# Expert down projection as three F32R products, with later row-number copies, a scatter without padding rows and an earlier first search

## The chip, the cores and the metric

The kernel runs on one core of a Trainium2 chip. The metric is the device time of one execution in microseconds. Three executions of the kernel before gave a median of 2249.87 us (2245.90 to 2253.77).

## What is computed

The reference is one layer of a decoder trunk over 1024 tokens of 1024 channels in float32: token mixers, a layer norm, a mixture of experts, a second layer norm. The change lies in the mixture of experts:

```python
N_EXPERTS = 64; TOP_K = 6; D_EXPERT = 256; D_MODEL = 1024
x = layer_norm(ALPHA * x + mix)                   # 1024 tokens
scores = sigmoid(x @ router_w.T)                  # (1024, 64)
gate, eidx = 6 experts of each token, weights that sum to 2.5
y[token] = shared(x)[token] + sum over its 6 experts e of
    gate * ((silu(x @ wg[e]) * (x @ wu[e])) @ wd[e])   # 1024 -> 256 -> 1024
x = layer_norm(ALPHA * x + y)
```

So there are 6144 pairs of a token and an expert. Each expert has 3 MB of weights: `wg` and `wu` of 1 MB each, and `wd` of 1 MB.

## The kernel before

**Stages.** The mixers and their merge fill the first 1100 us or so; they are not changed. `back` holds the rest: the output projection and first layer norm with the router (to about 1222 us), the tables of the routing and the shared expert of the first four token tiles (to 1275), the expert loop (to 2176), and a tail with the shared expert of the last four tiles (`shared_up(4)` to `shared_up(7)`, `tail_down`) and the second layer norm.

**Blocks.** The rows of each expert are cut into blocks of 128. There are 76 blocks, numbered b, with two buffer slots (s = b % 2). Block b passes through these steps:

- `one_hots(b)` (VectorE, L1987) compares positions with ranks; `find(b)` (TensorE, L1577) multiplies that with token numbers and weights; `rows(b)` (VectorE, L1992 to L2005) turns the result into row numbers `idx` and row weights. Rows past the expert's count get the number r + 1024, a padding row.
- `gather(b)` (GpSimd, L1429): an indirect DMA of the rows from `x1d`. It has a bound of S - 1, past which rows are not moved.
- `turn(b)` (TensorE, L1539) transposes the rows; ScalarE copies them out (L1739).
- `up(b)` (TensorE, L1550): eight float32 products of 512 columns, in two parts of four; ScalarE makes the silu (L1746), VectorE the product (`hide`, L2018).
- The transposes of `hidden` (TensorE, L1698), and a ScalarE copy to `hid_t` (L1824).
- `down(b)` (TensorE, L1564): four float32 products of 512 columns; copies of the two halves to `y_out` by ScalarE (L1835) and VectorE (L2034).
- The scatter (GpSimd, L1473): an indirect DMA that adds the 128 rows of `y_out` into `acc` in DRAM. It has no bound: `acc` has 128 rows more for the padding rows. Each waits until the one before has landed, as two experts may hold one token.

**Order.** Each engine runs a program of its own, written out by hand, and they meet in semaphores. TensorE's body of block b is: transposes of hidden(b), `up(b+1)` part 0, `find(b+3)`, `up(b+1)` part 1, `turn(b+2)`, `down(b)`. VectorE's is: `rows(b+3)`, `hide(b+1)`, `one_hots(b+4)`, the copy of half of y. At the end of `hide(b+1)` VectorE waits until scatter b-1 has landed, and copies the row numbers to `idx_out` (L2021). ScalarE's is: `hid_t`, silu of b+1, the copy of `turn(b+2)`, the copy of half of y. GpSimd's is: `gather(b+3)`, scatter b.

**Weights.** SyncE loads `w_gu` (both up matrices) and `w_d` of an expert into rings of four slots. The load for expert k+3 is issued when the last `up` of expert k-1 is done, that of `w_d` for k+2 when the last `down` of k-2 is done. `up_landed` and `down_landed` tell TensorE that a slot is filled.

**Before the loop.** TensorE interleaves the shared expert of tiles 0 to 3 with the tables. GpSimd adds each tile's result to the scaled x (L1452) and stores it to `acc` (L1454); only after the fourth store has landed does it issue `gather(2)`, which `turn(2)` waits for, and `down(0)` stands behind `turn(2)`. `find(0)` and `find(1)` stand behind the third shared transposes.

**After the loop.** The last two bodies are written out. Between them TensorE runs `shared_up(4)` (L1510), and in the last body `shared_up(5)` before `down`. VectorE runs `tail_hidden(4)` and `tail_hidden(5)` (L2049) before its own last body.

Of the kernel before, what the change touches and what calls it, by code (L numbers as in the profile page):

```python
# [18 lines left out]
P = 128  # L19
D = 1024  # L20
S = 1024
KD = D // P
NT = S // P
# [1202 lines left out]
def back(nc, d, c_at, merged, w_out, work, rings_at, half_merged, wo_in, piece_in, consts_moe, x1d, acc, x1, out, sem):  # L1226


    with ExitStack() as ctx:
# [6 lines left out]
        cst, rb, sh = sb('e_const', [P, consts_moe.shape[1]]), sb('rb', [P, E]), sb('sh', [P, 6144])  # L1236
# [6 lines left out]
        def const(name):  # L1243
# [17 lines left out]
        s_acc = y_out  # L1261
        x_gt = work[:, 2048:4096].rearrange('p (s k c) -> p s k c', s=2, c=P)
# [24 lines left out]
        scored, counted = sem('scored'), sem('counted')  # L1287
# [23 lines left out]
                  (ht_ready, 1))  # L1311
# [10 lines left out]
        def _(sp):  # L1322
# [60 lines left out]
            for t in range(NU, NT):  # L1383
                sp.wait_ge(x_scaled, t - NU + 1)
                sp.dma_start(acc[t * P:(t + 1) * P, :], x1_n[:, t, :]).then_inc(acc_rest, 16)
            sp.wait_ge(s_y, NU)
            load_up(2, 2)
            load_down(2, 2)
            up_landed(0, 0)
            up_landed(1, 0)  # L1390
# [3 lines left out]
            down_landed(0, 0)  # L1394
# [7 lines left out]
            for k in range(E - 4, E):  # L1402
                step(k, k % 4, k // 4)

# [16 lines left out]
        def _(pool):  # L1421
# [25 lines left out]
            for t in range(NU):  # L1447
                s = t % 2
                if t + 1 in (1, 3):
                    shared_hidden(t + 1)  # L1450
                pool.wait_ge(s_y, t + 1)
# [13 lines left out]
            def body(b, s, ahead=True):  # L1465
                if ahead:
# [3 lines left out]
                pool.wait_ge(so_ready, b + 1)  # L1470
# [3 lines left out]
                                        in_=y_out[:, s, :], in_offset=None, compute_op=ALU.add  # L1474
# [16 lines left out]
        def _(pe):  # L1491
# [13 lines left out]
            def shared_up(t, part=None):  # L1505
# [3 lines left out]
                for k in range(KD) if part is None else range(4 * part, 4 * part + 4):  # L1509
                    ins = pe.matmul(bank[s][:, :], turned_x1(t)[:, k, :], s_gu[:, k, :], start=k == 0, stop=k == KD - 1)  # L1510
# [45 lines left out]
            def down(b, s, e):  # L1556

                pe.wait_ge(d_landed, e + 1)
# [586 lines left out]
```

## Time and profile before

| | before |
|---|---|
| median of three executions | 2249.87 us |
| profiled execution, its own time | 2247.61 us |
| span of the profiled execution | 2245.6 us |
| TensorE busy | 95% of the span |
| mean granted TensorE clock | 0.98 |
| VectorE, ScalarE, GpSimd busy | 44%, 23%, 22% |
| DMA | 391.6 MB, 174 GB/s over the span; 297 GB/s from 1350 to 2150 us |

The profile is one execution. A trace row tells when an instruction began, how long it took and what its engine had waited for. In the chain of waits, pieces of TensorE are paced by the distance from one matmul to the next, and are thus shorter than the sum of the durations, since matmuls overlap. A float32 product appears as two matmul records.

### The profile page before, as it was taken

To read this page: it belongs to the slowest core of one execution; us is meant where nothing else is said; L and a number is where in the kernel's file an instruction comes from. 1 tells how busy PE (TensorE), PEld (TensorE's weight loads), DVE (VectorE), ACT (ScalarE), POOL (GpSimd) and SP (SyncE) were. 2 spreads that over 40 slices of the span, in tenths; PEclk is the share of its full clock that TensorE was granted. 3 is DMA by queue.
4 is the path that set the end of the run, shared out by engine and by line. 5 is a ranking of instruction groups with operands and counts; after the bars stand their busy time and mean duration, and the time that the engine had idled before them with its cause. 6 is when DMAs were issued, how large, how long until landed. Compare 5 with 4: busy or idle time off the path is not lost. (4 is left out here: it accounts for less than half of the span.)

```text
span 2245.6 us, 30409 instructions
## 1 busy us (share of the span) xinstructions
PE 2135.6 (95%) x9137; PEld 1340.0 (60%) x9138; DVE 984.2 (44%) x2409; ACT 525.6 (23%) x1056; POOL 493.0 (22%) x341
## 2 busy tenths in 40 slices
PE   7999999899999999689999799999999999999995
PEld 5887777677786666468455345455455555454542
DVE  2694525443076777388367222222222222222226
ACT  2111212342123444310132211211222112111213
POOL 2342232233132210012000312122222221222113
PEclk8999999999999999899999899999999999999998
DMA  5122221224322110377603578999888989888844
GB/s 174 47 67 89 71 66 29 80 52 101 102 80 74 48 43 17 106 234 241 227 28 132 196 227 278 331 329 336 293 291 283 327 287 325 280 288 294 261 83 159
DMA packets 162926, 391.62 MB, mean 174 GB/s; under 512 B 22272, under 2 KB 92193, under 8 KB 138144
## 3 DMA queue, kind: packets, MB, share of 16 engines
q1 hardware_dynamic: 127328, 294.88, 35.5%
q0 software_dynamic: 26304, 78.92, 16.4%
q10 hardware_dynamic: 9216, 16.78, 2.0%
q8 instruction: 49, 0.80, 0.2%
q14 instruction: 29, 0.24, 0.0%
HBM read 329.70 MB, written 75.50 MB: 180 GB/s over the span
## 5 line engine op out<-in xcount | busy, mean ns | idle before, releaser
L1550 PE MATMUL e_bank<-w_gu,work 128*128 x1216 | 553.1, 598 | 2.4 <-SPq L1338 1.7
L538 PE MATMUL a_bank<-x_hi,w_hi 128*128 128x512 f32 x928 | 375.7, 405 | 9.0 <-DVE x_lo L898 9.0
L538 PE MATMUL a_bank<-x_hi,w_lo 128*128 128x512 f32 x928 | 365.2, 394 | 0.0
L538 PE MATMUL a_bank<-x_lo,w_hi 128*128 128x512 f32 x928 | 364.9, 393 | 0.0
L1550 PEld LDWEIGHTS e_bank<-w_gu,work 128*128 128x128 f32 x1216 | 219.6, 190 | 222.2 <-issue 221.7
L1564 PE MATMUL e_bank<-w_d,norm 128*128 x608 | 274.9, 595 | 0.0
L1473 POOL DMA_INDIRECT acc<-work,idx_out x76 | 120.1, 1581 | 642.6 <-issue 613.6
L538 PEld LDWEIGHTS a_bank<-x_hi,w_hi 128*128 128x128 f32 x928 | 176.6, 190 | 50.4 <-issue 13.4
L538 PEld LDWEIGHTS a_bank<-x_hi,w_lo 128*128 128x128 f32 x928 | 176.3, 190 | 38.5
L538 PEld LDWEIGHTS a_bank<-x_lo,w_hi 128*128 128x128 f32 x928 | 176.7, 190 | 34.6 <-issue 0.5
L1564 PEld LDWEIGHTS e_bank<-w_d,norm 128*128 128x128 f32 x608 | 110.6, 192 | 110.8 <-issue 110.8
L481 POOL CAST w_hi<-w_raw 128x1024 fp32r<-128x1024 f32 x56 | 65.0, 1162 | 489.5 <-PE a_bank L538 489.5
L1746 ACT ACTIVATE norm<-e_bank 128x256 f32<-128x256 f32 x76 | 29.1, 383 | 500.3 <-PE e_bank L1550 500.3
L483 POOL TENSOR_TENSOR w_lo<-w_raw,w_hi 128x1024 fp32r<-128x1024 f32 x56 | 145.0, 2589 | 4.6
L1987 DVE TENSOR_TENSOR one_hot<-e_const,x 128x1024 bf16 x78 | 95.5, 1225 | 112.6 <-issue 112.6
L2018 DVE SCALAR_TENSOR_TENSOR norm<-e_bank,row_gate,norm 128x256 f32<-128x256 f32 x76 | 36.7, 484 | 236.4 <-ACT norm L1746 236.4
L1502 PE MATMUL e_bank<-work 128*128 128x512 f32 x256 | 113.1, 600 | 4.2 <-issue 4.2
L1539 PEld LDWEIGHTS e_bank<-e_const,work 128*128 128x128 f32 x608 | 79.4, 191 | 41.4 <-issue 36.1
L1429 POOL DMA_INDIRECT work<-x1d,idx x77 | 80.2, 1042 | 87.0 <-DVE idx L2005 47.3
L918 DVE SCALAR_TENSOR_TENSOR reg_b<-reg_b,conv_p 128x1024 f32<-128x1024 f32 x60 | 98.2, 1712 | 0.0
L836 ACT ACTIVATE reg_a<-a_bank 128x512 f32<-128x512 f32 (+2 forms) x106 | 58.5, 552 | 155.3 <-PE a_bank L545 153.7
L1739 ACT ACTIVATE work<-e_bank 128x512 f32<-128x512 f32 x152 | 82.5, 595 | 43.0 <-PE e_bank L1539 43.0
(331 smaller groups left out, 2442.8 us busy)
## 6 DMA issues: line engine op xcount, KB each, us to landing
w_d<-in_moe_wd SPq DMA_DIRECT2D x64, 1024.0 KB, 8.5
w_gu<-in_moe_wg SPq DMA_DIRECT2D x64, 1024.0 KB, 7.0
w_gu<-in_moe_wu SPq DMA_DIRECT2D x64, 1024.0 KB, 9.2
w_raw<-in_w_in SPq DMA_DIRECT2D x54, 512.0 KB, 3.8
gates<-gate_out ACTq DMA_DIRECT2D x64, 256.0 KB, 2.0
g_sb<-gates SPq DMA_DIRECT2D x16, 1024.0 KB, 6.2
work<-in_w_out SPq DMA_DIRECT2D x4, 1024.0 KB, 9.1
x<-in_x SPq DMA_DIRECT2D x8, 512.0 KB, 12.1
```

The lines of the kernel that those rows point to most:

```text
L481: pool.tensor_copy(w_hi[:, c % 2, :, :], w_raw[:, c % 2, :, :]).then_inc(w_hi_ready, 1)
L483: pool.tensor_tensor(w_lo[:, c % 2, :, :], w_raw[:, c % 2, :, :], w_hi[:, c % 2, :, :].bitcast(F32), ALU.subtract).then_inc(w_lo_ready, 1)
L538: ins = pe.matmul(bank[h][:, :], w[:, c % 2, k, :], x[:, k, cols], start=(k == 0 and j == 0), stop=(k == KD - 1 and j == 2))
L918: ins = dve.scalar_tensor_tensor(conv_y[:, c, :], conv_h[:, c, k:k + S], conv_p[:, c, k:k + 1], conv_y[:, c, :], ALU.mult, ALU.add)
L1429: pool.indirect_dma_start(out=x_g[:, s, :], out_offset=None, in_=x1d[:, :], in_offset=bass.IndirectOffsetOnAxis(ap=idx[:, s:s + 1], axis=0 ...
L1473: pool.indirect_dma_start(out=acc[:, :], out_offset=bass.IndirectOffsetOnAxis(ap=idx_out[:, s:s + 1], axis=0), in_=y_out[:, s, :], in_offs ...
L1502: ins = pe.matmul(bank[2 * (t % 2) + h][:, :], merged[:, k, t * P:(t + 1) * P], w_out[:, k, h * HALF:(h + 1) * HALF], start=k == 0, stop=k ...
L1539: ins = pe.transpose(bank[4 + k // 4][:, (k % 4) * P:(k % 4 + 1) * P], x_g[:, s, :].rearrange('p (c k) -> p k c', k=KD)[:, k, :], ident)
L1550: ins = pe.matmul(bank[s][:, :].rearrange('p (m f) -> p m f', m=2), x_gt[:, s, k, :], w_gu[:, bass.ds(e & 3, 1), :, k, :].rearrange('p a m ...
L1564: ins = pe.matmul(bank[2 + h][:, :], hid_t[:, j, :], w_d[:, bass.ds(e & 3, 1), j, h * HALF:(h + 1) * HALF].rearrange('p a f -> p (a f)'), ...
L1739: ins = act.activation(x_gt[:, s, 4 * h:4 * h + 4, :], bank[4 + h][:, :].rearrange('p (k c) -> p k c', k=4), ACT.Copy)
L1987: dve.tensor_tensor(one_hot[:, s, :, :], bcast(ranks, 1, NT), pos[:, :, bass.ds(e, 1)].broadcast_to([P, NT, P]), ALU.is_equal).then_inc(oh ...
```

## The change

- The shared expert's matrices are loaded a second time before the tail, into ring slots of the last experts (`tail_gu`, `tail_d`), and their old place `sh` is given to `d_hi`, `d_lo`, `h_hi` and `h_lo`, all of type F32R. (`tail_gu` is 2 MB, `tail_d` 1 MB.)
- `down(b)` becomes, for each of its four products, three F32R products: high x high, high x low, low x high. ScalarE copies `w_d` to `d_hi` (two copies of 128x1024) and the transposed hidden to `h_hi`; VectorE subtracts for `d_lo` (two of 128x1024) and `h_lo` (128x256). TensorE waits for `d_lo_ready` and `ht_ready`, and no longer loads the expert number for `down` into a register; ScalarE and VectorE now do.
- The copy of row numbers to `idx_out` moves from `hide(b+1)` to the end of body b, behind `one_hots(b+4)`, and waits for the scatter of b-2.
- The scatter gets the bound S - 1.
- `find(0)` and `find(1)` move forward, between the two parts of `shared_up(3)`, with the register loads; GpSimd makes each shared hidden product one tile earlier and issues `gather(0)` and `gather(1)` before it waits for tile 1's result; SyncE announces the first weights before it waits for the shared expert.

```diff
-        scored, counted = sem('scored'), sem('counted')
+        scored, tail_in = sem('scored'), sem('tail_in')
+        d_hi_ready, d_lo_ready, h_hi_ready = sem('d_hi_ready'), sem('d_lo_ready'), sem('h_hi_ready')
...
+            up_landed(0, 0)
+            up_landed(1, 0)
+            down_landed(0, 0)
             sp.wait_ge(s_y, NU)
             load_up(2, 2)
             load_down(2, 2)
-            up_landed(0, 0)
-            up_landed(1, 0)
             load_down(3, 3)
             sp.wait_ge(acc_rest, 16 * (NT - NU))
             load_up(3, 3)
-            down_landed(0, 0)
...
                 step(k, k % 4, k // 4)
+                if k == E - 3:
+                    sp.wait_ge(gu_blocks, blocks_until(E - 4) + 2)
+                    for i, name in enumerate(('sh_wg', 'sh_wu')):
+                        sp.dma_start(tail_gu[:, :, i * FE:(i + 1) * FE], d[name][0].rearrange('(k p) f -> p k f', p=P)
+                                     ).then_inc(tail_in, 16)
+                if k == E - 2:
+                    sp.wait_ge(gu_blocks, blocks_until(E - 3) + 2)
+                    sp.dma_start(tail_d, d['sh_wd'][0].rearrange('(k p) n -> p k n', p=P)).then_inc(tail_in, 16)
...
-                if t + 1 in (1, 3):
+                if t + 1 < NU:
                     shared_hidden(t + 1)
+                if t == 1:
+                    pool.wait_ge(x1_stored, 16 * NT)
+                    for k in range(2):
+                        gather(k, k)
                 pool.wait_ge(s_y, t + 1)
...
                 pool.dma_start(acc[t * P:(t + 1) * P, :], s_acc[:, s, :]).then_inc(acc_in[s], 16)
-                if t == 1:
-                    shared_hidden(2)
-                    pool.wait_ge(x1_stored, 16 * NT)
-                    for k in range(2):
-                        gather(k, k)
...
-                pool.wait_ge(so_ready, b + 1)
+                pool.wait_ge(so_ready, b + 2)
...
-                                        in_=y_out[:, s, :], in_offset=None, compute_op=ALU.add
+                                        in_=y_out[:, s, :], in_offset=None, bounds_check=S - 1, oob_is_err=False,
+                                        compute_op=ALU.add
                                         ).then_inc(scattered, 16)
...
-            def down(b, s, e):
-
-                pe.wait_ge(d_landed, e + 1)
+            def down(b, s):
+
+                pe.wait_ge(d_lo_ready, 2 * b + 2)
                 pe.wait_ge(ht_ready, b + 2)
...
                 for h in range(2):
+                    cols = slice(h * HALF, (h + 1) * HALF)
                     for j in range(2):
-                        ins = pe.matmul(bank[2 + h][:, :], hid_t[:, j, :],
-                                        w_d[:, bass.ds(e & 3, 1), j, h * HALF:(h + 1) * HALF
-                                            ].rearrange('p a f -> p (a f)'), start=j == 0, stop=j == 1)
+                        for i, (x, w) in enumerate(((h_hi, d_hi), (h_hi, d_lo), (h_lo, d_hi))):
+                            ins = pe.matmul(bank[2 + h][:, :], x[:, j, :], w[:, j, cols], start=j == 0 and i == 0,
+                                            stop=j == 1 and i == 2)
                 ins.then_inc(d_blocks, 1)
...
             shared_turn(1)
-            shared_up(3)
+            shared_up(3, 0)
+            n = trips(pe)
+            e_first = [expert_of(pe, blk) for blk in range(3)]
+            find(0, 0, e_first[0])
+            find(1, 1, e_first[1])
+            shared_up(3, 1)
             shared_down(1)
             shared_turn(2)
-            n = trips(pe)
-            find(0, 0, expert_of(pe, 0))
-            find(1, 1, expert_of(pe, 1))
             shared_down(2)
...
             body(2 * n, 0, n, ahead=False)
+            pe.wait_ge(tail_in, 48)
             shared_up(NU)
...
+            def down_high(b, e):
+
+                act.wait_ge(d_landed, e + 1)
+                act.wait_ge(d_blocks, b + 2)
+                for j in range(2):
+                    act.activation(d_hi[:, j, :], w_d[:, bass.ds(e & 3, 1), j, :].rearrange('p a f -> p (a f)'), ACT.Copy
+                                   ).then_inc(d_hi_ready, 1)
+
             def body(b, s, ahead1=True, ahead=True):
+                down_high(b, expert_of(act, b))
                 act.wait_ge(ht_done, b + 3)
-                act.wait_ge(d_blocks, b + 2)
-                act.activation(hid_t[:, :, :], bank[6][:, 0:2 * P].rearrange('p (j c) -> p j c', j=2), ACT.Copy
-                               ).then_inc(ht_ready, 1)
+                act.activation(h_hi, bank[6][:, 0:2 * P].rearrange('p (j c) -> p j c', j=2), ACT.Copy
+                               ).then_inc(h_hi_ready, 1)
...
-                dve.wait_ge(scattered, 16 * blk + 16)
-                dve.tensor_copy(idx_out[:, s:s + 1], idx_kept[:, s:s + 1]).then_inc(so_ready, 1)
+
+            def down_low(b, e):
+
+                for j in range(2):
+                    dve.wait_ge(d_hi_ready, 2 * b + j + 1)
+                    dve.tensor_tensor(d_lo[:, j, :], w_d[:, bass.ds(e & 3, 1), j, :].rearrange('p a f -> p (a f)'),
+                                      d_hi[:, j, :].bitcast(F32), ALU.subtract).then_inc(d_lo_ready, 1)
+                dve.wait_ge(h_hi_ready, b + 1)
+                dve.tensor_tensor(h_lo, bank[6][:, 0:2 * P].rearrange('p (j c) -> p j c', j=2), h_hi.bitcast(F32),
+                                  ALU.subtract).then_inc(ht_ready, 1)
 
             def body(b, s, ahead1=True, ahead=True):
+                down_low(b, expert_of(dve, b))
                 if ahead:
                     rows(b + 3, 1 - s)
...
                 if ahead:
                     one_hots(b + 4, s)
+                dve.wait_ge(scattered, 16 * b + 16)
+                dve.tensor_copy(idx_out[:, s:s + 1], idx_kept[:, s:s + 1]).then_inc(so_ready, 1)
                 dve.wait_ge(d_blocks, b + 3)
-                dve.wait_ge(scattered, 16 * b + 16)
                 dve.tensor_copy(y_out[:, s, HALF:D], bank[3][:, :]).then_inc(y_dve, 1)
```

## Rows read from the trace of the kernel before

**Rows 1.** Part 1 of the page: busy us (share of the span) x instructions.
```profile
PE 2135.6 (95%) x9137; PEld 1340.0 (60%) x9138; DVE 984.2 (44%) x2409; ACT 525.6 (23%) x1056; POOL 493.0 (22%) x341
```
**Rows 2.** Chain of waits, 1950 to 1963 us: start us, us, what.
```profile
1950.29 3.44 PE e_bank L1564 x8
1953.73 0.23 PE e_bank L1698 x2
1953.95 3.44 PE e_bank L1550 x8
...
1957.57 3.54 PE e_bank L1550 x8
1961.11 0.89 PE e_bank L1539 x8
```
**Rows 3.** Timeline, silu copies of two blocks: start us, us, engine line op [idle <-releaser].
```profile
1308.85 0.38 ACT L1746 ACTIVATE norm<-e_bank 128x256 f32<-128x256 f32 x1 [6.43 <-PE e_bank L1550]
...
2161.86 0.38 ACT L1746 ACTIVATE norm<-e_bank 128x256 f32<-128x256 f32 x1 [6.43 <-PE e_bank L1550]
```
**Rows 4.** Timeline, F32R products of the mixer stage.
```profile
299.96 0.39 PE L538 MATMUL a_bank<-x_hi,w_hi 128*128 128x512 f32 x1
...
302.90 0.39 PE L538 MATMUL a_bank<-x_lo,w_hi 128*128 128x512 f32 x1
```
**Rows 5.** Chain of waits, 1500 to 1530 us.
```profile
1508.64 7.75 DMA acc<-work,idx_out
...
1516.41 0.07 DVE idx_out L2021
...
1520.88 2.93 DMA acc<-work,idx_out
```
**Rows 6.** DMA queues, 1450 to 1550 us: packets, MB, share of 16 engines.
```profile
q1 hardware_dynamic: 3547, 25.77, 63.2%
q0 software_dynamic: 2429, 7.13, 36.7%
```
**Rows 7.** Issue to landing: the scatter (L1473), then the gather (L1429).
```profile
DMA to landing us min/median/max: 6.0/7.2/9.9
...
DMA to landing us min/median/max: 2.9/7.5/11.4
```
**Rows 8.** One line's instructions: copy (L1186) and subtraction (L1206) to F32R, ns min/median/max.
```profile
L1186 ACT ACTIVATE y_hi<-work x8: 1037/1058/1915, 945.7 to 963.5; 128x1024 fp32r<-128x1024 f32 x6, 128x2048 fp32r<-128x2048 f32 x2
L1206 DVE TENSOR_TENSOR y_lo<-work,y_hi x8: 1218/1226/3975, 946.8 to 965.9; 128x1024 fp32r<-128x1024 f32 x6, 128x2048 fp32r<-128x2048 f32 x2
```
**Rows 9.** Timeline of one block, 1956 to 1962 us.
```profile
1958.35 0.27 DVE L2005 TENSOR_SCALAR idx<-idx_f,found,e_const 128x1 int32<-128x1 f32 x1
1960.89 1.04 POOL L1429 DMA_INDIRECT work<-x1d,idx  x1 [3.19 <-issue]
```
**Rows 10.** Timeline of the last one-hots before the loop, then the chain of waits.
```profile
1242.90 1.22 DVE L1987 TENSOR_TENSOR one_hot<-e_const,x 128x1024 bf16 x1 [0.65 <-issue]
...
1259.47 6.44 PE e_bank L1529 x8
...
1274.95 9.11 DMA acc<-work
...
1285.85 9.26 DMA work<-x1d,idx
```
**Rows 11.** Timeline in the tail, end of `shared_up(5)`.
```profile
2190.48 3.60 PE L1564 MATMUL e_bank<-w_d,norm 128*128 x8
2190.74 0.38 ACT L1813 ACTIVATE norm<-e_bank 128x256 f32<-128x256 f32 x1 [6.44 <-PE e_bank L1510]
2191.22 0.42 DVE L2049 TENSOR_TENSOR norm<-e_bank,norm 128x256 f32<-128x256 f32 x1 [6.68 <-ACT norm L1813]
```
**Rows 12.** Timeline, a small VectorE instruction beside GpSimd's addition.
```profile
1272.32 2.33 POOL L1452 TENSOR_TENSOR work<-work 128x1024 f32<-128x1024 f32 x1 [1.97 <-ACT work L1804]
...
1272.52 2.15 DVE L2002 SCALAR_TENSOR_TENSOR idx_f<-found,e_const 128x1 f32<-128x1 f32 x1
```

More of the change, by code:

```diff
@@ L1235, in back @@
         scores = sb('scores', [P, NT, E])
-        cst, rb, sh = sb('e_const', [P, consts_moe.shape[1]]), sb('rb', [P, E]), sb('sh', [P, 6144])
+        cst, rb = sb('e_const', [P, consts_moe.shape[1]]), sb('rb', [P, E])
+        sh_at = (nc.sbuf_base + 31) // 32 * 32
+        sh = sb('sh', [P, 6144])
+        assert nc.sbuf_base == sh_at + 4 * 6144
         x1_late = sb('x1_late', [P, NT - NU, KD, P])
@@ L1261, in back @@
         s_acc = y_out
+        tail_gu = w_gu[:, 0, :, :, :].rearrange('p m k f -> p (m k f)').rearrange('p (k f) -> p k f', k=KD)
+        tail_d = w_gu[:, 1, 0, :, :].rearrange('p k f -> p (k f)').rearrange('p (k n) -> p k n', k=2)
+        d_hi, d_lo, h_hi, h_lo = (nc.alloc_sbuf_tensor_at(name, [P, 2, n], F32R, offset=sh_at + at) for name, n, at in (
+            ('d_hi', D, 0), ('d_lo', D, 8 * D), ('h_hi', P, 16 * D), ('h_lo', P, 16 * D + 8 * P)))
+        d_hi, d_lo, h_hi, h_lo = d_hi[:, :, :], d_lo[:, :, :], h_hi[:, :, :], h_lo[:, :, :]
         x_gt = work[:, 2048:4096].rearrange('p (s k c) -> p s k c', s=2, c=P)
@@ L1310, in back @@
         CREDIT = ((gu_blocks, 2), (d_blocks, 2), (h_ready, 2), (ht_done, 2), (y_act, 1), (y_dve, 1), (xt_done, 1),
-                  (ht_ready, 1))
+                  (ht_ready, 1), (so_ready, 1))
         def trips(eng):
@@ L1509, in shared_up @@
                 for k in range(KD) if part is None else range(4 * part, 4 * part + 4):
-                    ins = pe.matmul(bank[s][:, :], turned_x1(t)[:, k, :], s_gu[:, k, :], start=k == 0, stop=k == KD - 1)
+                    ins = pe.matmul(bank[s][:, :], turned_x1(t)[:, k, :], (s_gu if t < NU else tail_gu)[:, k, :], start=k == 0,
+                                    stop=k == KD - 1)
                 if part != 0:
@@ L1636, in tail_down @@
                         ins = pe.matmul(bank[2 + 2 * (t % 2) + h][:, :], tail_t[:, t % 2, j, :],
-                                        s_d[:, j, h * HALF:(h + 1) * HALF], start=j == 0, stop=j == 1)
+                                        tail_d[:, j, h * HALF:(h + 1) * HALF], start=j == 0, stop=j == 1)
                 ins.then_inc(s_down, 1)
@@ L1682, in _ @@
             turn(0, 0, 16)
-            find(2, 0, expert_of(pe, 2))
+            find(2, 0, e_first[2])
             for part in range(2):
-                up(0, 0, expert_of(pe, 0), part)
+                up(0, 0, e_first[0], part)
             pe.wait_ge(s_y, NU)
@@ L1708, in body @@
                     up(b + 1, 1 - s, e_up, 1)
-                e_down = expert_of(pe, b)
                 if ahead:
                     turn(b + 2, s, 16 * i + 32)
-                down(b, s, e_down)
+                down(b, s)
             turn(1, 1, 16)
@@ L1999, in rows @@
                     dve.wait_ge(xt_done, blk)
+                    if not isinstance(blk, int):
+                        dve.wait_ge(so_ready, blk - 2)
                     keep_rows(s)
@@ L2026, in body @@
                 elif ahead1:
+                    dve.wait_ge(so_ready, b + 1)
                     keep_rows(1 - s).then_inc(idx_ready, 1)
```

## The prediction

> **What bounds the kernel now.** I read page part 1 first: TensorE is busy 95% of the span, the next engine half as much [rows 1]. The share alone doesn't say whether the expert loop waits for something, so I read the chain of waits over one block next [rows 2]. The pieces touch each other: 3.44 us for `down`, 0.23 for the hidden transposes, 3.44 and 3.54 for the two parts of `up`, with 0.18 for `find` between them, 0.89 for `turn`. Their starts run from 1950.29 to 1961.11 + 0.89 = 1962.00, a period of 11.71 us, and all of it is TensorE. How often is a block longer? The silu copies mark each block; from 1308.85 to 2161.86 lie 72 periods [rows 3], 853.0 us, where 72 x 11.706 would be 842.8. So TensorE paces the loop, and all other waits in it cost 10.2 us together.
>
> Those 10.2 us come from a ring that is as long as the block. In the chain around 1500 us a scatter is issued at 1508.64 and takes 7.75 us; then VectorE copies row numbers at 1516.41, does `one_hots` and its half of y, and GpSimd issues the next scatter at 1520.88, 12.24 us after the one before [rows 5]. Just there the DMA engines are full: 63.2% of their time for weights and 36.7% for gather and scatter [rows 6]. So the block has three limits close together: TensorE at 11.71, the scatter ring at about 12.2 when transfers are slow, and the transfers themselves. The question is which of them is next once TensorE is faster.
>
> **The products.** F32R products of 512 columns start 0.226 us apart in the mixer stage: 13 steps from 299.96 to 302.90 [rows 4]. The new `down` has 4 x 3 = 12, so 2.71 us in place of 3.44 [rows 2]: 0.73 us less. For 76 blocks that is 55.5 us, all on the path. Bounds: none of these sits in a mixture of float32 and F32R instructions of this form; if each `down` paid one unhidden start of a product (0.39 - 0.23 = 0.16 us more), 12 us would be lost. I take none, as the two row types are alike in shape.
>
> **What feeds them.** Per block ScalarE makes two copies of 128x1024 at 1.05 us and VectorE two subtractions at 1.22 us [rows 8], and 0.42 us for `h_lo` (as the tail's product of that size [rows 11]). All instructions of this can begin only when the previous `down` is done, since `d_hi` and `d_lo` have one buffer. Counted from the start of `down(b-1)`: it ends at about 3.0 (2.71 and 0.3 until the next engine starts), the y copies are issued, a register load for the expert number takes some 0.8 (estimate: from 1516.41 to the next scatter's issue are 4.5 us [rows 5]; less 1.22 for `one_hots` [rows 10], 0.7 for the y copy and 1 to issue, 1.6 are left for two such loads), so `d_hi` is made from 3.8 to 5.9, `h_hi` to 6.2, `d_lo` from 4.9 to 7.3, `h_lo` to 7.7. TensorE wants them at 10.98, after transposes, `up`, `find` and `turn`. The cover is 3.3 us, so I cost this at nothing. If it is gone, each microsecond past it is a microsecond per block. Behind the new waits on VectorE stands `rows(b+3)`, about 1.0 us (to 8.7), then `hide(b+1)`, which can't run before the silu at about 10.5: 1.8 us of room. Behind `rows` stands the gather. Before, row numbers were ready at 1958.62 and `down` began at 1961.83 by its first record, 3.2 us later; now it is 2.3. And `turn(b+3)` wants the rows one period later, which is 0.73 shorter. The gather had 11 to 13 us between its issue (1960.89 [rows 9]) and its `turn`; it will have about 10 to 11.5. It lands after 7.5 us in the median, 11.4 at most [rows 7]: most fit, a few don't. I cost these at 3 us in all (bounds 0, and 1 us for each of the 45 or so blocks that run with full DMA engines).
>
> **The copy of row numbers.** Moved behind `one_hots` and waiting for the scatter of b-2, it leaves the ring. What is left of the ring is the landing, 7.2 to 9.9 us [rows 7], and about 1 us to issue, against 10.98. `so_ready` now comes one block later for GpSimd, but 0.15 us before the y copy, which it waits for anyway. So the 10.2 us mostly go: 10.2 less the 3 for gathers is a gain of 7.
>
> **No padding rows.** Scatters carry 76 x 128 = 9728 rows, of which 6144 are real. The transfers between 1450 and 1550 us took 36.7 us of all engines for 7.13 MB, 5.1 us per MB [rows 6]; 3584 rows of 4 KB are 14.7 MB, so about 75 us of the DMA engines' time, 1.0 us per block. None of it is on the path now. Its worth is that it keeps the transfers out of the way: in that stretch a block with new weights takes 63.2/8.19 = 7.7 us for weights (25.77 MB at 3.15 MB per expert are 8.19 experts) and 36.7/8.24 = 4.5 us for rows, together 12.2; without some 45 padding rows it is 11.3 by this price, against a new TensorE period of 10.98. Two facts soften that: 76 blocks share 64 loads, and the ring of four slots lets the loads run two or three experts ahead. Over the loop the sum is 64 x 7.7 + 76 x 3.5 = 759 us against 76 x 10.98 = 834. I cost it at nothing, with the rival below.
>
> **Before the loop.** Now TensorE gets to `find(0)` at 1256.21, because it first waits for GpSimd's hidden product of tile 2, which stands behind tile 1's result. In the new order that product needs only the silu of tile 2, and the searches can start as soon as the one-hots are there: the second were made from 1242.90 to 1244.1 [rows 10]. Stepping through the new order with the durations of the trace (`down` of a tile 3.44 us and half an `up` 3.54 [rows 2], ScalarE's copies 1.05 [rows 8], GpSimd's addition 2.33 [rows 12]), TensorE does find(0), find(1) by 1246, the second half of `shared_up(3)` by 1249.5, `shared_down(1)` by 1253, (2) by 1258, (3) by 1263.5, and GpSimd stores tile 3 at 1267.4, where it was 1274.95 [rows 10]. That is 7.5 us earlier; part of it is `shared_down(2)`, which took 6.44 us at a reduced clock after idling [rows 10] and would take 3.44. The chain behind it, 9.11 us for the store and 9.26 for `gather(2)` [rows 10], doesn't change: I find no edit in it. Bounds: 3 (if the searches wait longer for registers) to 10.
>
> **The tail.** Here the change adds a wait. VectorE does `tail_hidden(5)` before its last body, and that needs the end of `shared_up(5)`; the subtractions for the last block stand behind it. `shared_up(5)` ends at 2190.5, VectorE starts its product at 2191.22 [rows 11], ends it at 2191.6, then 0.4 of register load not covered, 2 x 1.22 and 0.42: 2194.9. TensorE was to start `down` at 2190.48, and everything behind it (three more `shared_up` or `tail_down` groups and the last layer norms) moves with it. It costs 4.3 us (bounds 2 to 6). The reload of 3 MB falls into a stretch with free DMA engines and has two blocks, over 20 us, to land: nothing.
>
> **Sum.** 55.5 (products) + 7 (ring, less late gathers) + 7.5 (start) - 4.3 (tail) = 65.7 us. From the profiled execution's 2247.6 us, which is 0.1% under the median, that gives 2182; I say 2183.
>
> **The rivals.**
> *Transfers bind.* Padding rows are left out of the scatter as they are of the gather, but may still cost something each, or loads and rows may be slower together than I added. If a block with new weights still takes 12.0 us wherever the engines are full (about 525 us of the loop, 44 blocks), 44 x (12.0 - 10.98) = 45 us are lost: 2228. For it: the queues' shares add to 99.9% [rows 6]. Against it: 57 of the 72 periods are the bare 11.71 even so. With half of the padding's price saved it is some 22 us, 2205. Chance 0.13, most of it near the smaller loss.
> *Gathers come late.* `turn` waits about 1 us in each of those 44 blocks: 2224. For it: the margin shrinks by 1.6 us, and a gather issued behind the next weights' load queues behind 2 MB. Against: median 7.5. Chance 0.10.
> *VectorE becomes the bound, and the kernel slower.* One step decides: the two subtractions of `d_lo` run beside GpSimd's descriptor work for the scatter, issued at about 4.5. If VectorE is shut out as it was beside GpSimd's addition, where a small instruction took 2.15 us [rows 12] against 0.27 for one of like size [rows 9], each by its rest of 1.6 to 2, VectorE's ring (about 9.2 us of work and waits that can't move) gets to 12.5 with both and with the scatter's wait, 0.8 more than now: 2247.6 + 76 x 0.8 = 2308 less 10 for start and ring, about 2300. It decides from 2.5 us more per block, since 1.8 is room and the TensorE gain is 0.73. The Trainium skill, page "SBUF — State Buffer", section "Who interferes with whom", speaks for this rival: a VectorE instruction with two SBUF inputs contends with a GpSimd instruction that reads SBUF, and whoever starts first holds the port throughout; `d_lo` has two such inputs, and by that rule alone the outcome hangs on whether descriptor work reads SBUF long enough. For the addition the trace agrees (2.15 us) [rows 12]; no row shows a long VectorE instruction beside an indirect DMA's issue. Chance 0.04.
> *The products don't pay:* mixed with float32 they start 0.29 us apart, so `down` takes 3.44 again: 2183 + 55 = 2238. Chance 0.03.
>
> **How the numbers follow.** Forecast 0.70, between 2170 and 2198 (start and tail at their bounds, gathers at 0 or 13 us); the rivals as above. A range of 2168 to 2224 holds the forecast, the transfers' rival but for its end, and the gathers' rival: about 9 in 10 by these chances, as the bounds of the start and the gathers make it. A measurement of this kernel tells 0.3% (7 us) from no change. Faster: 0.70 + 0.13 + 0.10 + 0.02 of the products' = 0.95, taken down to 0.93 as rivals can add up; slower 0.05; same 0.02.
>
> **What would show it.** Right: the L1564 piece 2.7 us long with 12 instructions; periods of 10.98 in most blocks; VectorE's copy to `idx_out` with no wait; the queue of gather and scatter at some 25 MB less 10 or more; the fourth store to `acc` near 1267; a wait of about 4 us before the last `down`. Wrong: TensorE waiting in `turn` for DMA (gathers, or transfers if SyncE's loads land late too), or in L1564 for VectorE (the slower rival).

## The result, and the profile after

| | median | range | runs |
|---|---|---|---|
| before | 2248.3 us | 2245.9 to 2253.8 | 4 |
| after | 2190.9 us | 2189.1 to 2195.7 | 4 |

The ratio is 0.9747, with a 95% interval from 0.9726 to 0.9767: 2.5% faster. That is 8 us more than the 2183 that was forecast, inside the range. The profiled execution took 2190.8 us (span 2188.6), against 2247.6 before: 56.8 us less, where the sum said 65.7.

To see where they went, I cut both spans at the same places: the copy to `table`, the silu copy of the third block, and the silu copy 72 periods on, that of the last block but one.

| stretch, us | before | after | difference |
|---|---|---|---|
| up to `table` (no edit lies there) | 1238.2 | 1239.1 | +0.9 |
| `table` to the third silu: the start | 70.65 | 65.95 | -4.7 |
| 72 periods of the loop | 853.0 | 795.7 | -57.3 |
| from there to the end | 83.8 | 87.9 | +4.1 |

The page of after: part 1, then the queues (packets, MB, share of 16 engines), then three groups of part 5.

```profile
PE 2079.4 (95%) x9441; PEld 1391.2 (64%) x9442; DVE 1180.7 (54%) x2637; ACT 677.5 (31%) x1209; POOL 500.5 (23%) x341
...
q0 software_dynamic: 26304, 64.27, 12.0%
...
L2056 DVE TENSOR_TENSOR d_lo<-w_d,d_hi 128x1024 fp32r<-128x1024 f32 x152 | 179.4, 1222 | 128.3 <-ACT d_hi L1847 127.7
L1489 POOL DMA_INDIRECT acc<-work,idx_out x76 | 127.1, 1673 | 434.9 <-issue 253.7
...
L1847 ACT ACTIVATE d_hi<-w_d 128x1024 fp32r x152 | 152.3, 1049 | 33.6 <-issue 27.9
```

VectorE has nearly 200 us more work and ScalarE 150 us more than in [rows 1], and TensorE is still busy 95% of a span that is 57 us shorter. A share of busy time can't tell 2246 from 2189 us; the chain can. The chain of waits of after over one block (start us, us, what), as [rows 2] was of before:

```profile
1305.88 2.75 PE e_bank L1584 x12
1308.63 0.23 PE e_bank L1719 x2
1308.86 3.44 PE e_bank L1568 x8
1312.30 0.18 PE e_bank L1596 x8
1312.48 3.54 PE e_bank L1568 x8
1316.02 0.88 PE e_bank L1557 x8
1316.89 2.75 PE e_bank L1584 x12
```

The pieces touch, as before, and the only one that changed is `down`: 2.75 us with 12 instructions, 3.44 with 8 before. Twelve steps of 0.226 would be 2.71 [rows 4]. The period of this block is 11.01. Of the 72 periods, 69 lie between 11.00 and 11.06 with a mean of 11.03; three near 1492 to 1538 us took 11.21, 11.40 and 12.01.

What feeds the products, in the timeline of after (start us, us, engine, line, operation, [idle before <- releaser]), in a block whose `down` starts at 1682.23 and the next at 1693.29:

```profile
1684.79 0.15 DVE L2074 COPY idx_out<-idx_kept 128x1 int32<-128x1 int32 x1
...
1686.55 2.00 ACT L1847 ACTIVATE d_hi<-w_d 128x1024 fp32r x2 [0.58 <-issue]
1687.01 1.58 POOL L1489 DMA_INDIRECT acc<-work,idx_out  x1 [5.06 <-issue]
...
1687.84 2.36 DVE L2056 TENSOR_TENSOR d_lo<-w_d,d_hi 128x1024 fp32r<-128x1024 f32 x2 [1.85 <-ACT d_hi L1847]
...
1690.11 0.41 DVE L2059 TENSOR_TENSOR h_lo<-e_bank,h_hi 128x256 fp32r<-128x256 f32 x1
...
1691.08 0.27 DVE L2036 TENSOR_SCALAR idx<-idx_f,found,e_const 128x1 int32<-128x1 f32 x1
...
1692.42 1.04 POOL L1446 DMA_INDIRECT work<-x1d,idx  x1 [3.82 <-issue]
...
1693.10 0.48 DVE L2049 SCALAR_TENSOR_TENSOR norm<-e_bank,row_gate,norm 128x256 f32<-128x256 f32 x1 [1.75 <-ACT norm L1767]
...
1693.29 0.48 PE L1584 MATMUL e_bank<-d_hi,h_hi 128*128 128x512 f32 x1
```

Counted from the start of `down`: `d_hi` from 4.3 to 6.3 us (forecast 3.8 to 5.9), `d_lo` from 5.6 to 8.0 (4.9 to 7.3), `h_lo` done at 8.3 (7.7), the row numbers at 9.1 (8.7), and `hide` still finds VectorE idle for 1.75 us (1.8). The copy to `idx_out` has no wait. TensorE wants `h_lo` at 11.06, so 2.8 of the 3.3 us of cover are there.

The start, in the chain of waits of after; it answers to [rows 10].

```profile
1245.97 1.07 PE e_bank L1596 x8
1247.04 6.00 PE e_bank L1527 x8
1253.04 3.45 PE e_bank L1547 x8
...
1268.11 2.33 POOL work L1473
...
1270.74 9.04 DMA acc<-work
...
1281.58 9.97 DMA work<-x1d,idx
...
1291.59 1.97 PE e_bank L1557 x8
1293.56 4.06 PE e_bank L1584 x12
```

The fourth store starts at 1270.74: 4.2 us earlier than before, not 7.5. The second half of `shared_up(3)` (L1527 x8) took 6.00 us, and I had put 3.5 for it. From 1242.9 to 1247.0 TensorE had only `find(0)` and `find(1)` to do and waited ahead of both for VectorE, and the granted clock of 1240 to 1250 us is 0.75; full clock, 1.00, came only in the stretch from 1260. Then a store and a gather end one behind the other, as before, and `turn` and `down` behind them run in a stretch with a clock of 0.69, 1290 to 1300.

The tail, in the chain of waits of after; it answers to [rows 11].

```profile
2121.22 6.88 PE e_bank L1527 x16
...
2128.19 0.39 ACT norm L1834
...
2129.69 0.07 DVE d_lo L2056
...
2130.83 1.23 DVE d_lo L2056
2132.06 0.43 issue
2132.49 4.60 PE e_bank L1584 x12
```

TensorE ends `shared_up(5)` at 2128.1, and `down` of the last block starts 4.4 us later: the wait that was forecast at 4.3. But then this `down` takes 4.60 us where the others take 2.75. The granted clock of 2130 to 2140 us is 0.83.

### The profile page after: what moved, and what is told of

The parts are those of the page before. It is cut to its first block, busy times and chain, and to the rows that moved or that the text cites. A ratio compares the mean times of both kernels' runs of the same rounds, so it can differ in the third digit from the quotient of the medians.

```text
span 2188.6 us, 32088 instructions
## 1 busy us (share of the span) xinstructions
PE 2079.4 (95%) x9441; PEld 1391.2 (64%) x9442; DVE 1180.7 (54%) x2637; ACT 677.5 (31%) x1209; POOL 500.5 (23%) x341
## 3 DMA queue, kind: packets, MB, share of 16 engines
q0 software_dynamic: 26304, 64.27, 12.0%
## 4 chain that ended last, share of the span: by engine, by line
PE 46%; DMA 2%; DVE 2%; issue 1%; ACT 0%; DVEq 0%; POOL 0%; ACTq 0%; POOLq 0%
PE e_bank L1568 22%; PE e_bank L1584 9%; PE e_bank L1519 5%; PE e_bank L1557 3%; PE e_bank L1527 2%; DMA work<-x1d,idx 2%; PE e_bank L1719 1%; PE e_bank L1547 1%; PE e_bank L1618 1%; PE e_bank L1596 1%; DMA acc<-work 0%; PE e_bank L1628 0%; DVE ln_stats L2128 0%; DVE x L2113 0%; DVE x L2124 0%
## 5 line engine op out<-in xcount | busy, mean ns | idle before, releaser
L2056 DVE TENSOR_TENSOR d_lo<-w_d,d_hi 128x1024 fp32r<-128x1024 f32 x152 | 179.4, 1222 | 128.3 <-ACT d_hi L1847 127.7
L1489 POOL DMA_INDIRECT acc<-work,idx_out x76 | 127.1, 1673 | 434.9 <-issue 253.7
L1847 ACT ACTIVATE d_hi<-w_d 128x1024 fp32r x152 | 152.3, 1049 | 33.6 <-issue 27.9
L1584 PE MATMUL e_bank<-d_hi,h_hi 128*128 128x512 f32 x304 | 127.3, 419 | 4.4 <-DVE d_lo L2056 4.4
L1584 PE MATMUL e_bank<-d_hi,h_lo 128*128 128x512 f32 x304 | 120.9, 398 | 0.0
L1584 PE MATMUL e_bank<-d_lo,h_hi 128*128 128x512 f32 x304 | 119.6, 393 | 0.0
```

The lines of the kernel that those rows point to most:

```text
L1489: pool.indirect_dma_start(out=acc[:, :], out_offset=bass.IndirectOffsetOnAxis(ap=idx_out[:, s:s + 1], axis=0), in_=y_out[:, s, :], in_offs ...
L1584: ins = pe.matmul(bank[2 + h][:, :], x[:, j, :], w[:, j, cols], start=j == 0 and i == 0, stop=j == 1 and i == 2)
L1847: act.activation(d_hi[:, j, :], w_d[:, bass.ds(e & 3, 1), j, :].rearrange('p a f -> p (a f)'), ACT.Copy).then_inc(d_hi_ready, 1)
L2056: dve.tensor_tensor(d_lo[:, j, :], w_d[:, bass.ds(e & 3, 1), j, :].rearrange('p a f -> p (a f)'), d_hi[:, j, :].bitcast(F32), ALU.subtract ...
```

## The experiments

Eleven kernels; each ratio is to runs of the kernel before on the same chip. `twice1`, `twice2` and `best` ran on another chip than the other experiments, one on which the kernel before took 2245.7 us. Start, loop and end are the stretches of the table above, in the profiled executions.

### `pad`: the padding rows are scattered again

```diff
-  in_=y_out[:, s, :], in_offset=None, bounds_check=S - 1, oob_is_err=False,
-  compute_op=ALU.add
+  in_=y_out[:, s, :], in_offset=None, compute_op=ALU.add
```

> The changed kernel (2190.9 us) with the bound of the scatter taken out again, so that all 128 rows of a block are scattered. My sum gave the bound no worth of its own: then 2191 to 2193 us. But the scatters of the changed kernel land after 9.0 us in the median with 80 rows, near the period of 11.05, so with 3584 rows more (about 1 us of all DMA engines per block) I now lean to a few late scatters and gathers: 2196 to 2206 us, with TensorE waiting in turn for gathers. The rival that transfers bind as soon as they are whole gives 22 to 45 us: 2213 to 2236.

Measured: 2192.4 us, ratio 0.9743 (0.9712 to 0.9774): no different from after (0.9747). The busy time of each engine, the clock, the DMA share and GB/s of `pad`, in a stretch of the loop:

```profile
1450.00:1550.00 100.00, 99.83 (x418) 59.55 (x417) 53.26 (x118) 39.10 (x64) 27.91 (x19) 1.00 1.02 358
```

With DMA engines full (a share of 1.02), TensorE is still busy 99.83 of 100 us. The list of waits of `pad` has no wait of TensorE for a load of expert weights in the whole span. So the edit is worth nothing here, as the prediction costed it; my later lean to 2196 to 2206 us did not come true. The rival that transfers bind falls: even with all padding scattered they don't.

### `ring`: the copy to `idx_out` at the old place, with the products

```diff
                 (end of hide(blk))
+                dve.wait_ge(scattered, 16 * blk + 16)
+                dve.tensor_copy(idx_out[:, s:s + 1], idx_kept[:, s:s + 1]).then_inc(so_ready, 1)
                 (y copy, behind one_hots)
-                dve.wait_ge(scattered, 16 * b + 16)
-                dve.tensor_copy(idx_out[:, s:s + 1], idx_kept[:, s:s + 1]).then_inc(so_ready, 1)
```

(with the waits on `so_ready` as they were before)

> The changed kernel with the copy of row numbers put back behind hide(b+1), where it waits for scatter b-1. If the copy only costs what it cost before (10 us in 76 blocks) this is 2201 us. My theory of the ring says more: landing 7.2 to 9.0 us, then 1.6 us of register loads, 1.2 of one-hots, 0.7 of y copy and 1 to issue make 11.7 to 13.5 us from one scatter to the next, against a TensorE period of 11.05, so every block is paced by the ring: 2191 + 76 x 0.7 to 2.5 = 2244 to 2380 us, with TensorE waiting before the transposes or in find, and most of the gain of the products gone.

Measured: 2246.6 us, ratio 0.9997 (0.9974 to 1.0019). All of the gain is gone. The loop took 849.3 us, 11.80 a period in the mean; 46 of the 72 periods are over 11.15 us, single ones up to 16.9. The chain of waits of `ring` has left TensorE:

```profile
1500.75 6.93 DMA acc<-work,idx_out
1507.70 0.06 DVE idx_out L2050
...
1509.31 0.09 DVE one_hot L2016
...
1510.46 0.69 DVE work L2074
...
1512.25 4.23 DMA acc<-work,idx_out
...
1524.95 6.24 DMA acc<-work,idx_out
```

From one scatter to the next: landing, copy, `one_hots`, half of y, issue, next landing. It is the ring of [rows 5]. Before, it and TensorE's 11.71 were so near to each other that it showed only in some periods (16 of 72, by 0.07 to 2.14 us; the prediction counted 15). With the products TensorE's period is 11.0, and the ring, which no product shortens, sets the pace in most blocks.

### `f32down`: `down` in float32 again, all else as after

```diff
-  pe.wait_ge(d_lo_ready, 2 * b + 2)
+  pe.wait_ge(d_landed, e + 1)
...
-  for i, (x, w) in enumerate(((h_hi, d_hi), (h_hi, d_lo), (h_lo, d_hi))):
-      ins = pe.matmul(bank[2 + h][:, :], x[:, j, :], w[:, j, cols], ...)
+  ins = pe.matmul(bank[2 + h][:, :], hid_t[:, j, :], w_d[...], start=j == 0, stop=j == 1)
```

(and no `down_high`, no `down_low`)

> The changed kernel with down in float32 as before and without the copies and subtractions for it; all else is changed. If the products alone give 11.71 - 11.01 = 0.70 us per block, 76 x 0.70 = 53 us come back, less the wait of the last down (4.4 us) and its slow clock (1.9 us), which go: 2236 to 2239 us, with nearly all periods at 11.71. If transfers or the ring held the changed kernel instead of TensorE, less comes back: under 2225 us.

Measured: 2235.5 us, ratio 0.9937 (0.9917 to 0.9957). In the chain of waits the `down`s of `f32down` are

```profile
1949.64 3.44 PE e_bank L1583 x8
...
1961.35 3.44 PE e_bank L1583 x8
```

11.71 apart, and all 72 periods are: the loop took 842.9 us, the 72 x 11.706 = 842.8 that the prediction worked out from [rows 2]. The excess of 10.2 us is gone to the last tenth. The end took 83.8 us, as before. So the 4.1 us that after has more come with `down_low` and the products; `tail` below shows that it is `down_low`'s place behind `tail_hidden(5)`.

### `copy_alone`: only the copy to `idx_out` moved, in the kernel before

```diff
                 (end of hide(blk))
-                dve.wait_ge(scattered, 16 * blk + 16)
-                dve.tensor_copy(idx_out[:, s:s + 1], idx_kept[:, s:s + 1]).then_inc(so_ready, 1)
                 (y copy, behind one_hots)
+                dve.tensor_copy(idx_out[:, s:s + 1], idx_kept[:, s:s + 1]).then_inc(so_ready, 1)
```

(with the waits on `so_ready` and `scattered` as the change has them)

> The kernel before (2248.5 us) with only the copy of row numbers moved behind one_hots. If the ring of scatter, copy and one-hots made the 10.2 us over the bare 11.71 us periods, all 72 periods come to 11.71 and the time is 2238 to 2239 us. If full DMA engines made them by themselves, the long periods stay: 2246 to 2249 us.

Measured: 2239.8 us, ratio 0.9951 (0.9930 to 0.9973); the loop 842.9 us, every period 11.71. Alone the move gives the 10.2 us of the loop, and padding has no part in it. Put beside `ring`, this is the main finding. The move is worth 853.0 - 842.9 = 10 us with float32 products and 849.3 - 795.7 = 54 us with F32R ones. The products are worth 853.0 - 849.3 = 4 us of loop without the move (ring against before, the bound and the start differing too) and 842.9 - 795.7 = 47 with it. Neither has a price of its own: the sum 55.5 + 10 holds for the pair. The scatter's landing has no fixed price either. With the move alone it took 8.8 us in the median (5.9 to 10.8), where it was 7.2 [rows 7] with the same rows; no run shows why.

### `bound_alone`: only the padding rows left out, in the kernel before

```diff
+  bounds_check=S - 1, oob_is_err=False,
```

> The kernel before with only the bound on the scatter. The ring stays, but its landing gets shorter where transfers are full: 3584 rows fewer are about 1 us of all DMA engines per block, so 12.2 us becomes 11.2 to 11.7, under TensorE's 11.71, and most of the 10.2 us go too: 2239 to 2243 us. If landing time doesn't follow the number of rows, nothing changes: 2248 us.

Measured: 2248.7 us, ratio 0.9978 (0.9954 to 1.0002); the loop 854.2 us, no shorter than before (853.0). A miss: I had thought that a lighter scatter lands sooner and so shortens the ring. The queue of gather and scatter did become lighter, from 43.4 MB and 35.5% of the engines' time in 1400 to 2000 us to 32.6 MB and 25.4%. The landing hardly became shorter; the chain of waits of `bound_alone` has at 1504.88 a scatter that takes 9.29 us, and the copy right behind it:

```profile
1504.88 9.29 DMA acc<-work,idx_out
...
1514.19 0.07 DVE idx_out L2022
```

In the 69 blocks in which the copy to `idx_out` waits for a landing, it comes 4.8 to 10.0 us after the scatter's issue, 7.3 in the mean; before, 6.0 to 9.9 in 70 blocks, with a mean of 7.4. Why so little is open: the weights' transfers lie beside the scatter either way, and no run separates the two.

### `tail`: `tail_hidden(5)` behind the last `down_low`

```diff
                 down_low(b, expert_of(dve, b))
+                if not ahead1:
+                    dve.wait_ge(ht_done, b + 3)
+                    tail_hidden(5)
...
-            dve.wait_ge(ht_done, 2 * n + 4)
-            tail_hidden(5)
```

> The changed kernel with tail_hidden(5) moved behind the subtractions of the last block on VectorE. The wait of 4.4 us before the last down goes, and with it the drop of the clock after it (down took 4.6 us in place of 2.7): 2191 - 6 = 2184 to 2186 us. Rival: the end hangs on the last scatter and the loads of acc, so the wait was covered: 2189 to 2191 us.

Measured: 2184.8 us, ratio 0.9709 (0.9679 to 0.9739). The end took 81.7 us, 6.2 less than after. In its chain of waits:

```profile
2121.55 6.87 PE e_bank L1527 x16
2128.42 2.78 PE e_bank L1584 x12
```

No wait, and `down` at its usual length; the granted clock of 2130 to 2140 us is 1.00. So the 6.2 us are the 4.4 of the wait and 4.60 - 2.78 = 1.8 of the slower clock behind it.

### `clock`: the searches of blocks 0 and 1 apart

```diff
-            find(0, 0, e_first[0])
-            find(1, 1, e_first[1])
             shared_up(3, 1)
+            find(0, 0, e_first[0])
             shared_down(1)
+            find(1, 1, e_first[1])
```

> The changed kernel with find(0) behind the whole of shared_up(3) and find(1) behind shared_down(1), so that TensorE doesn't wait for one-hots and row numbers between 1243 and 1246 us. In the changed kernel the second half of shared_up(3) took 6.0 us after that wait, at a lower granted clock, where it takes 3.5 at the full one. If the wait is what costs (2.5 us of waiting, 2.5 us of slow clock), the fourth store to acc comes 4 to 6 us earlier and the time is 2185 to 2187 us. If GpSimd or ScalarE set the pace there, nothing: 2190 to 2192 us.

Measured: 2190.85 us, ratio 0.9729 (0.9695 to 0.9763). By the medians of four executions each (2187.2 to 2192.0 here, 2189.1 to 2195.7 for after) this is no gain, where 4 to 6 us were expected. In the profiled executions the start is 62.3 us against 65.95, 3.7 less, and the fourth store starts at 1266.96 in place of 1270.74. The granted clock of 1240 to 1250 us is 1.00 in place of 0.75, and the half `up` is back at its usual length, so the cause is right. A new wait comes a step later, in the timeline of TensorE:

```profile
1256.74 0.44 PE L1538 MATMUL e_bank<-e_const,norm 128*128 128x128 f32 x2 [2.00 <-POOL norm L1456]
1257.75 4.51 PE L1547 MATMUL e_bank<-sh,norm 128*128 128x512 f32 x6 [0.56 <-ACT norm L1813]
```

TensorE is now ahead of GpSimd, whose hidden product stands behind the gather's issue and an addition, and waits there for 2.0 us; this `shared_down(2)` takes 5.38 us in the chain of waits, where it was 3.69.

### `gather_first`: `gather(2)` ahead of the waits for the stores

```diff
+            n = trips(pool)
+            gather(0, 2)
             (waits on acc_in and acc_rest)
-            n = trips(pool)
...
-            gather(0, 2)
```

> The changed kernel with gather(2) issued by GpSimd before it waits for the stores to acc, not behind them. turn(2) waited until 1291.59 us, 5.1 us after up(1) had ended, and then turn(2) and the first down ran at a lower clock (2.4 us more). If only GpSimd's order held the gather, both go: 2183 to 2185 us. If the gather lands late anyway, behind 7 MB of weights issued at the same time: 2189 to 2191 us.

Measured: 2185.4 us, ratio 0.9706 (0.9671 to 0.9741); the start took 58.46 us, 7.5 less than after, as expected. The gather reads `x1d`, which the stores don't touch; only the order on GpSimd's queue had put it behind them. Its chain of waits has no transfer left there:

```profile
1277.07 0.90 PE e_bank L1557 x8
...
1286.99 0.88 PE e_bank L1557 x8
1287.87 2.78 PE e_bank L1584 x12
```

`turn` starts at 1286.99 where it was 1291.59, and `down` takes 2.78 us, not 4.06, since TensorE no longer waits ahead of it.

### `twice1` and `twice2`: more work on VectorE, to measure the cover

One or two more subtractions a block of 128x1024, whose result nobody reads, ahead of those for `d_lo` (operands are shortened here).

```diff
+                    if j < 2:            (twice1: j < 1)
+                        dve.tensor_tensor(waste[j], w_d[:, e & 3, j, :], d_hi[:, j, :], ALU.subtract)
```

> The changed kernel with one more subtraction of 128x1024 on VectorE in each block, into a place that nothing reads, ahead of d_lo (1.22 us more per block). The prediction's cover: h_lo is ready 2.7 us before down wants it, and hide(b+1) comes 1.7 us after the row numbers, so VectorE has room for this. But the gather is issued 1.2 us later, 9.8 us before its turn at most, against landings of 8.2 us in the median and 12.1 at most. I expect 0 to 10 us more, 2191 to 2201 us, all of it waits of TensorE for gathers in turn. If VectorE were the bound already, each block would pay 1.22 us: 2284 us.

Measured: 2198.1 us, ratio 0.9777 (0.9739 to 0.9814). The loop is 4.3 us longer, the end 1.8.

> The same with two more subtractions (2.45 us per block). h_lo is then ready 0.3 us before down, hide(b+1) comes 0.7 us late, which TensorE doesn't see (the transposes come 2.7 us later), but the gathers are issued at most 8.6 us before their turn, about their median landing. I expect TensorE to wait for gathers in about half the blocks, 1 to 2 us each: 2220 to 2270 us. If VectorE's chain to h_lo is what ends the cover, TensorE waits in down for d_lo instead; if the cover of 3.3 us was all that mattered, 2191 us.

Measured: 2211.5 us, ratio 0.9836 (0.9795 to 0.9876), below what I expected. The loop is 12.7 us longer, 0.18 a block for 2.4 us of added work; the end 3.7. Who waits for whom in `twice2` (us in total, times, longest):

```profile
POOL work L1447 <- PE e_bank L1558: 171.1, 36, 6.0
...
PEld e_bank L1558 <- DMA work<-x1d,idx: 39.3, 44, 6.1
...
PEld e_bank L1585 <- DVE d_lo L2060: 8.7, 2, 7.5
```

`down` (L1585) waits for `d_lo` only in the last two blocks, and in none of the 72 periods: the cover of 2.8 us takes 2.4 more. What goes first is the gather. `rows` stands behind `d_lo` on VectorE, so the row numbers come 2.4 us later; `turn` (L1558) waits for the gather 44 times, in after 10 times, and a gather in its turn waits 36 times for a `turn` to free its buffer (L1447). These rows are of weight loads, which run ahead of the matmuls. Of the matmuls of `turn` 14 waited for a gather: one for 5.2 us before the loop (in after it is 5.2 too), the others for 8.2 us together. That is most of the loop's 12.7; the rest was not separated.

### `best`: `tail`, `clock` and `gather_first` together

> The changed kernel with three edits together: tail_hidden(5) behind the last subtractions, find(0) and find(1) placed so that TensorE doesn't wait, and gather(2) ahead of the wait for the stores. The tail edit alone gave 6 us; with 4 to 6 us and 6 to 7.5 us for the others, if they add: 2171 to 2176 us.

Measured: 2175.6 us, ratio 0.9677 (0.9640 to 0.9715). It beats both kernels, the changed one by 15 us (by 0.7% when the ratios are compared, as the chips differ). The start took 55.0 us (65.95), the end 81.7 (87.9), the loop 796.2 (795.7). Its start is 3.4 us shorter than that of `gather_first`: so much is the order of `clock` worth here. Its last `down` takes 2.78 us.

## Why the prediction was right or wrong

**What bounds the kernel, and the ring.** Right, and `ring` shows how much rested on it. The prediction costed the move at 10.2 less 3. As a difference from before, that is correct. It did name the ring at 12.2 us when transfers are slow, but it didn't say that without the move the 55.5 us of the products would have stayed out: the terms of the sum are not independent.

One figure of the step "What is left of the ring is the landing, 7.2 to 9.9 us" grew. In after the scatters (L1489) land so after their issue:

```profile
DMA to landing us min/median/max: 2.7/9.0/11.5
```

In 25 of the 76 blocks the next scatter waits for that landing. At the longest period two issues lie 11.97 us apart (1511.97 and 1523.94). TensorE lost little by it here, but the ring of landing and issue is nearly as long as its new period of 11.03, so a further cut of TensorE's work should meet it first. That is an estimate from these rows; no run tests it.

**The products.** The mechanism holds, its size was off. `down` is 2.75 us, not 2.71: the first product starts 0.32 us ahead of the second and the others are 0.23 apart. The period fell by 11.71 - 11.03 = 0.68, not by 0.73: 48.7 us over the 72 periods where 52.6 were forecast, 3.9 less. The rival that they don't pay fell with the 2.75 us of `down` in the chain.

**Late gathers.** Taken at 3 us. The three longer periods are 34.6 - 3 x 11.03 = 1.5 us over. At the longest, `turn` waits for a gather that took 12.1 us to land (median 8.2, against 7.5 in [rows 7]). So ring and gathers gave 10.2 - 1.5 = 8.7 where I had 7. With the products' 48.7 this makes the 57.3 us of the loop (but for rounding); the forecast for the same 72 periods was 59.6.

**The start.** 7.5 was taken, of bounds 3 to 10; with one `down` in that stretch 8.2, and it gave 4.7. The step that failed is "TensorE does find(0), find(1) by 1246, the second half of `shared_up(3)` by 1249.5". The time 1246 was nearly right: `find(1)` ends at 1247.04. But from 1242.9 to 1247.0 TensorE did nothing but the two searches, idle for 0.54 and 1.51 us ahead of them, and the half `up` behind them ran slow: 6.00 us for 3.5, in a stretch with a granted clock of 0.75. I had noted the same effect in the trace of before (6.44 us for `shared_down(2)`) and counted its end as a gain, but not that the new order makes a wait of its own. `clock` shows the cause by removing it: 3.7 us of the start go, against a wait of 2.05 and 2.5 of slow clock, as its order brings a wait of its own. The step "The chain behind it ... doesn't change" has the other 1.1 us of the 3.5 that are missing: from the fourth store to `turn` it took 20.85 us for 20.2 (the gather 9.97 for 9.26), and `turn` 1.97 for 1.52.

**The tail.** The step "the subtractions for the last block stand behind it" was right, with 4.4 us for 4.3. Left out was what follows a wait of TensorE of that length: `down` took 4.60 us for 2.75. `tail` gives back both.

**Padding rows.** Right at nothing, by `pad`. Their price in the DMA engines' time was near: 1.0 us a block was forecast, and `bound_alone` has 600 us x (35.5% - 25.4%) = 61 us for 51 blocks, 1.2. The bytes fell by 78.9 - 64.3 = 14.6 MB. The rival of binding transfers is out for this kernel, by `pad`.

**The slower rival.** VectorE was to be shut out beside the scatter's issue. Had it happened, `d_lo` would have been longer than 1.22 us. Over all 152 it is 1212/1224/1276 ns (min/median/max), and 70 of them begin within a scatter's issue, as at 1687.84 above; none of these took over 1.23 us. It is GpSimd that waits, when it comes second. In 61 blocks GpSimd's issue began first (or met no `d_lo`) and took 1.55 to 1.62 us. In 15 blocks the subtractions were already under way, and 12 of these issues took 1.77 to 2.60, as in this one of the timeline of after:

```profile
1742.70 2.36 DVE L2056 TENSOR_TENSOR d_lo<-w_d,d_hi 128x1024 fp32r<-128x1024 f32 x2 [1.59 <-ACT d_hi L1847]
1742.79 2.59 POOL L1489 DMA_INDIRECT acc<-work,idx_out  x1 [5.35 <-DMA acc<-work,idx_out]
```

The issue grows by what was left of the subtraction when it began, less 0.13 us: 1.01 us here, where 1.14 were left, and so, to 0.01, in 13 of the 14 blocks with 0.16 us or more left. (In the 14th, at 1865.43, the subtraction had begun 0.02 us earlier; the issue took 1.58 us and the subtraction 1.28.) So GpSimd is held until the subtraction has ended. In `f32down`, which has no `d_lo`, none of the 76 took over 1.63.

The Trainium skill, page "SBUF — State Buffer", section "Who interferes with whom", has a VectorE instruction with two SBUF inputs contend with a GpSimd instruction that reads SBUF, by an exclusive lock, and the order of issue decide who blocks. The trace agrees for GpSimd as the second (up to 1.0 us more). For VectorE as the second it shows no wait in 70 subtractions, and which part of the issue reads SBUF no run shows. The same section infers that a `tensor_tensor` doesn't stall descriptor generation; here it holds up the instruction that issues the scatter. So only the harmless outcome shows here: GpSimd had sat idle for 5 us ahead of its issues at 1687.01 and 1742.79, and TensorE set the pace.

**The miss of 8.9 us** (65.7 forecast, 56.8 measured in the profiled executions) is then: start 3.5, loop 59.6 - 57.3 = 2.3, end 2.0 (forecast 4.3 less three `down`s of 0.73, +2.1; measured +4.1), and 0.9 in stages that no edit touches, whose length varied from 1238.2 to 1244.0 us between these twelve kernels and before. The sum is 8.7; the spans differ by 57.0 us where the executions' own times differ by 56.8. Some 4 us of it are one thing: TensorE's slower clock behind its waits, 2.5 in the start and 1.9 in the tail.

## What to carry to other kernels

Before you add up the gains of edits, ask for each what the loop's period would be with it alone. Two rings of nearly equal length (here 11.7 and up to 12.2 us) can make each edit worth little by itself (10 and 4 us of the loop here) and the pair worth far more than the two together (57); the experiment that undoes one part of the finished change shows this better than the one that adds one part to the old kernel. Where an edit makes TensorE wait outside the loop (4.4 us here), add what the work behind the wait takes at the lower clock, from a row of the trace; and look at what stands on an in-order queue between a transfer's issue and its data being ready, since an issue that needs nothing from the waits ahead of it can be moved ahead of them (7.5 us of the start in `gather_first`).

## What the runs showed of the hardware

- After 4.1 us with two searches and 2.05 us of waits (1242.9 to 1247.0), and after a wait of 4.4 us (2128.1 to 2132.5), TensorE's next work ran at the lower level for a while: mean granted clocks of 0.75 (1240 to 1250 us) and 0.83 (2130 to 2140 us), between the levels of 1.2 GHz (0.5) and 2.4 GHz (1.00). It cost 2.5 and 1.9 us; `clock`, without the first, and `tail`, without the second, have 1.00 in these stretches.
- A scatter without its padding rows lands hardly sooner: 7.3 us in the mean against 7.4 (`bound_alone` and before), although the queue moved a quarter fewer bytes (32.6 MB for 43.4). The count of its packets is 26304 with and without them: in the traces of `bound_alone` and after, 3584 packets of 4096 bytes, one for each padding row, have become packets of 8 bytes.
- The DMA engines can be full (a share of 1.02 at 358 GB/s) without TensorE losing anything (99.83 of 100 us, `pad`); here the weight loads are issued two to three experts ahead, and no run has them later.
- An indirect DMA's issue on GpSimd that begins while a VectorE subtraction with two inputs in SBUF is running is held until that has ended: it takes 1.58 us and what was left of the subtraction, less 0.13 us (up to 1.0 us more, 13 blocks of after). The other way round, 70 subtractions that began within an issue took 1.21 to 1.23 us, as alone.
